# ScalarE instead of GpSimd writes the high parts of the product weights in an encoder layer's recurrence

## The chip, the core and the metric

The kernel is one program on one core of a Trainium2 chip. A core has TensorE (PE, with its weight loads shown as PEld), VectorE (DVE), ScalarE (ACT), GpSimd (POOL) and SyncE (SP), which here only starts transfers. The metric is the time of one execution on the device in microseconds, the median of several runs.

## What is computed

One layer, depth 1, batch 1, 1024 positions, 1024 channels, all float32. A single projection of x feeds a windowed attention, a recurrent branch and two merge gates:

```python
proj = einsum('bsd,de->bse', x, w_in) + b_in
q, k, v, g_attn, x_rnn, g_rnn, m_attn, m_rnn = split(proj)
attn = _window_attention(rope(q), rope(k), v, sink) * silu(g_attn)
xc = _centred_depthwise_conv(x_rnn, conv_w, conv_b)
rnn = _bidirectional_rglru(xc, ...) * silu(g_rnn)
merged = sigmoid(m_attn) * (attn @ w_branch_attn) + sigmoid(m_rnn) * (rnn @ w_branch_rnn)
x = layernorm(ALPHA * x + merged @ w_out + b_out)
```

The recurrence, for ten blocks of 128 channels and two directions:

```python
r = sigmoid(xb @ wa + ba); i = sigmoid(xb @ wx + bx)
log_a = -8 * r * softplus(-lam)
a = exp(log_a); u = sqrt(-expm1(2 * log_a)) * (i * x)
h = a * h + u      # forward over the positions, and backward; both are summed
```

## The kernel before

**Products in three parts.** Every matrix is split into a high part (the value as TensorE's fp32r type holds it) and a low part (the value less its high part). A product is high by high, high by low and low by high: three matmuls of 128 x 128 by 128 x 512. Weights arrive by DMA in `raw` or `raw_half`, one instruction makes `w_hi` and a second, a subtraction on POOL, makes `w_lo`.

**Stages.** Opening projection and attention run first, then (from about 430 us) the recurrence's first two blocks in plain form, then, from 461 us to 820 us, the stage that the change touches, and at the end the branch products, the output projection and the LayerNorm.

**The stage of the change.** Two units of 128 output columns are computed together as a "twin". By sums of the moving matrix that were made earlier, and sums of the weights, a twin takes seven half products instead of eight (Strassen's scheme with Winograd's sums). There are 16 twins (`TWINS`), so 112 half products, numbered n = 7q + i: twin q, product i from 0 to 6. One product is 12 matmuls (`product`, L1067 to L1082). Twins whose units are merge gates (`MERGES`) alternate with those that project x and the gate of a coming block.

The loop is over the blocks b = 2 to 9. In block b PE runs (L1143 to L1154): `gates(b, 0)`, product 0 of the block's twin q, `gates(b, 1)`, products 1 to 6 of q, then products 0 to 6 of the merge twin m. The two gate steps are 12 matmuls each, so a block has 16 such slots. Block 2 runs four products of q ahead of `gates(b, 1)`. Block 9 has no twin q, only m. Below, "q6" is product 6 of a block's twin q, "m0" product 0 of its merge twin, and so on.

**Weights of a product.** There are six landing places for raw halves (`half_slot`) and four for split weights (`w_slot`). A high part may be written once product n-3 has begun (`product_begun`, L1436 for ACT and L760 for POOL). The tuple `BY_ACT` says which of the 112 high parts ACT makes (`high_weights`, L1432, an ACTIVATE copy, counted in `act_hi_done`); all others are made by POOL in `split_half` (L763). POOL makes every low part (`low_weights`, L750), in the order of n. PE waits for it at L1070. SP loads the next raw half into a place when its low part is done (L606).

Before the change `BY_ACT` names products 2 to 9, and products 4, 5 and 6 of each merge twin but the last.

**What ACT does beside.** ACT's instructions for a block are written out by hand in a fixed order (L1546 to L1616): `early_copy(q, number)` takes partial products out of PSUM, number 3 after product 6; `sigmoids(b, 0)` and `(b, 1)` evacuate the gates; `decay_tanh`, `decay_exp`, `decay_square` and `roots` build the recurrence's coefficients; `conv_begin` and `conv_high` serve the next block's convolution; `merge_gate` applies the sigmoid of a merge gate and stores it by DMA; `sigmoid_of` makes the sigmoid for the gate of the branch. ACT changes its function table three times a block (ACT_TABLE_LOAD).

**What DVE does.** Also in fixed order (L1987 to L2026): `twin_sum` puts parts of a twin together (it waits for `early_done`), `gated_input`, `conv_tap`, `one_less_decay`, `scan_input`, `silu_of` (it waits for `sigmoid_of`), `scans` (two TENSOR_TENSOR_SCAN), `gated_sum`, which ends a block (`rnn_done`), and ACT's `sigmoids(b + 1, 0)` waits for that.

Both orders are coupled: ACT waits for DVE at `merge_gate`, `conv_begin` and `sigmoids`; DVE waits for ACT at `silu_of`, `one_less_decay`, `scan_input` and `twin_sum`.

Of the kernel before, what the change touches and what calls it, by code (L numbers as in the profile page):

```python
# [109 lines left out]
PLAIN = 1  # L110
TWINS = []
# [5 lines left out]
MERGES = tuple(q for q, twin in enumerate(TWINS) if twin[0][0] == "merge")  # L117
# [4 lines left out]
FIRST_PRESUM = 4  # L122


BY_ACT = (2, 3, 4, 5, 6, 7, 8, 9) + tuple(7 * q + i for q in MERGES[:-1] for i in (4, 5, 6))
ORDER = ((0, 0), None, (0, 1), None, (1, 1), None, None)
SUM_AT = {1: 0, 3: 1, 5: 3, 6: 2}

# [52 lines left out]
def encoder_layer(nc, x_t, x_rows, stream, small, tables, sink, b_out, ln_gain, ln_bias, out):  # L181
# [4 lines left out]
    with ctx:  # L186
# [521 lines left out]
        def _(pool):  # L708
# [43 lines left out]
            def split_half(n):  # L752

                pool.wait_ge(half_landed[n % N_SLOTS], 16 * (n // N_SLOTS + 1))
                if n in BY_ACT:
                    pool.wait_ge(act_hi_done, BY_ACT.index(n) + 1)
                    low_weights(n, half_slot(n % N_SLOTS))
# [462 lines left out]
        def _(act):  # L1220
# [130 lines left out]
            def conv_high(b):  # L1351
                act.wait_ge(convolved, b + 2)
                copy(conv_hi[:, :], conv[:, :]).then_inc(conv_hi_done, 1)
# [25 lines left out]
            def decay_tanh(b):  # L1379

                for d in range(2):
                    act.wait_ge(gate_freed[d], b * 2 + 3)
                    nc.scalar.activation(root[d][:, :], decay[d][:, :], ACT.Tanh,
                                         scale=rate[:, ds(b + d * RNN_BLOCKS, 1)]).then_inc(act_tanh, 1)

            def decay_exp(b, d):

                act.wait_ge(act_tanh, b * 2 + d + 1)
                nc.scalar.activation(decay[d][:, :], decay[d][:, :], ACT.Exp,
                                     scale=nrate[:, ds(b + d * RNN_BLOCKS, 1)]).then_inc(act_decay, 1)  # L1390

            def decay_square(b, d):

                act.wait_ge(act_decay, b * 2 + d + 1)
                if d == 1:
                    act.wait_ge(one_less, b * 2 + 1)
                elif b:
                    act.wait_ge(state_stored, 16 * b)
                nc.scalar.activation(square[:, :], decay[d][:, :], ACT.Square).then_inc(squared, 1)  # L1399
# [22 lines left out]
            def early_copy(q, number):  # L1422

                i, bank, at = ((0, 0, 0), (1, 2, 1), (3, 0, 2), (6, 0, 0))[number]
                act.wait_ge(product_done, 7 * q + i + 1)
                if number == 3:
                    act.wait_ge(twin_done, 4 * q + 1)
                elif q:
                    act.wait_ge(twin_done, 4 * (q - 1) + (4, 3, 2)[number])
                copy(early[:, at, :], twin_banks(q)[bank]).then_inc(early_done, 1)  # L1430

            def high_weights(q, i):  # L1432

                n = 7 * q + i
                act.wait_ge(half_landed[n % N_SLOTS], 16 * (n // N_SLOTS + 1))
                act.wait_ge(product_begun, max(1, n - 2))  # L1436
                copy(w_slot(n)[0], half_slot(n % N_SLOTS)).then_inc(act_hi_done, 1)

            def merge_gate(q, number):

                d, at = MERGES.index(q), number % 2
                gate_no, half = ((0, 0), (0, 1), (1, 1), (1, 0))[number]
                act.wait_ge(twin_done, 4 * q + number + 1)
                nc.scalar.activation(stage_out[:, at, :], stage_out[:, at, :], ACT.Sigmoid).then_inc(merge_gated, 1)
                act.wait_ge(merge_gated, 4 * d + number + 1)
                col = d * SEQ + half * HALF
                act.dma_start(merges[gate_no, :, col:col + HALF], stage_out[:, at, :])\
                    .then_inc(merge_stored[at], 16)
# [97 lines left out]
            for b in range(PLAIN + 1, RNN_BLOCKS):  # L1546
                last_one = b == RNN_BLOCKS - 1
                q, m = twin_of(b), merge_of(b)
                merge_before = merge_of(b - 1)
                if merge_before is not None:  # L1550
                    early_copy(merge_before, 3)
                if b == PLAIN + 1:
                    early_copy(q, 0)
                act.wait_ge(rnn_done, b)
                sigmoids(b, 0)
                if b == PLAIN + 1:
                    store_state(PLAIN)
                    early_copy(q, 1)
                    early_copy(q, 2)
                if merge_before is not None:  # L1560
                    merge_gate(merge_before, 2)
                    merge_gate(merge_before, 3)
                if q is not None and b > PLAIN + 1:
                    early_copy(q, 0)
                if last_one:
                    early_copy(m, 0)
                if not last_one:
                    conv_begin(b + 1, None)
                sigmoids(b, 1)
                if q is not None and b > PLAIN + 1:  # L1570
                    early_copy(q, 1)
                if last_one:
                    early_copy(m, 1)
                decay_tanh(b)
                decay_exp(b, 0)
                if not last_one:
                    decay_square(b, 0)
                decay_exp(b, 1)
                if b > PLAIN + 1:
                    early_copy(m if last_one else q, 2)  # L1580
                if last_one:
                    h_high(0)
                    h_high(1)
                    decay_square(b, 0)
                    merge_gate(m, 0)
                else:
                    conv_high(b + 1)
                decay_square(b, 1)
                if q is not None:
                    early_copy(q, 3)  # L1590
                if last_one:
                    merge_gate(m, 1)
                    early_copy(m, 3)
                    h_high(2)
                    h_high(3)
                roots(b)
                if last_one:
                    merge_gate(m, 2)
                    merge_gate(m, 3)
                    sigmoid_of(b)  # L1600
                    h_high(4)
                    h_high(5)
                    store_state(b)
                    for t in range(6, RNN_BLOCKS):
                        h_high(t)
                    break
                early_copy(m, 0)
                high_weights(m, 4)
                sigmoid_of(b)
                early_copy(m, 1)  # L1610
                high_weights(m, 5)
                high_weights(m, 6)
                early_copy(m, 2)
                merge_gate(m, 0)
                store_state(b)
                merge_gate(m, 1)  # L1616
# [609 lines left out]
```

## Time and profile before

| | |
|---|---|
| median of 3 runs | 1028.35 us (1027.28 to 1028.55) |
| the profiled execution | 1026.91 us, of which the span of its instructions 1025.1 us |
| busy: PE, PEld | 1005.0 us (98%), 831.5 us (81%) |
| busy: DVE, ACT, POOL | 687.3 us (67%), 476.4 us (46%), 650.5 us (63%) |
| granted TensorE clock, mean | 0.999 |
| HBM traffic | 112.55 MB read, 47.19 MB written |
| from 480.75 to 820.31 us | gate steps and products of blocks 2 to 9 |

The trace gives, for each engine, when an instruction ran and what its wait was for. Matmuls overlap: one of 128 x 512 shows 0.39 us, while the next starts 0.227 us after it. A busy PE in the table is therefore not a measure of its speed; the distance of starts is. In the busy shares of the whole span the stages are mixed: POOL is busy for three to six tenths of most slices of the attention, and for nearly all of the stage of the change.

### The profile page before, as it was taken

What the parts mean: (1) busy time and instruction counts of PE and PEld (TensorE: products, weight loads), DVE (VectorE), ACT (ScalarE), POOL (GpSimd) and SP (SyncE); (2) the same over time, 40 slices, a digit from 0 to 9 for tenths busy, and PEclk for the clock granted to TensorE, in tenths of its full rate; (3) what the DMA queues carried; (4) which work ended last, traced back from release to release, by engine and by line L of the source; (5) the groups of instructions that cost most, each with busy time, mean ns of one, the idle gap of its engine ahead of it and who ended that gap; (6) DMA issues with size and microseconds to landing.
All of it is one profiled execution on the core that took longest, in us unless ns stands there. A gap on an engine that the chain in (4) does not pass through costs nothing. (4 is left out here: it accounts for less than half of the span.)

```text
span 1025.1 us, 13044 instructions
## 1 busy us (share of the span) xinstructions
PE 1005.0 (98%) x4617; PEld 831.5 (81%) x4617; DVE 687.3 (67%) x776; ACT 476.4 (46%) x700; POOL 650.5 (63%) x399
## 2 busy tenths in 40 slices
PE   8999999999999999999999999999999999999997
PEld 6888888888888888888777788787887878888885
DVE  4946665603556653739788776978878588839756
ACT  4054455211554464775748566574855751102021
POOL 5654535545644534447999999999999733485223
PEclk9999999999999999999999999999999999999999
DMA  8264333575433431455352434435243788937012
GB/s 329 95 246 168 130 103 124 206 249 173 144 121 113 143 125 54 180 188 171 96 159 69 153 107 139 120 117 164 84 144 85 237 304 325 333 104 294 1 49 116
DMA packets 69605, 160.45 MB, mean 157 GB/s; under 512 B 7344, under 2 KB 7728, under 8 KB 69424
## 3 DMA queue, kind: packets, MB, share of 16 engines
q1 hardware_dynamic: 60624, 137.13, 40.6%
q10 hardware_dynamic: 8928, 22.64, 5.7%
q8 instruction: 31, 0.51, 0.2%
q14 instruction: 22, 0.18, 0.1%
HBM read 112.55 MB, written 47.19 MB: 156 GB/s over the span
## 5 line engine op out<-in xcount | busy, mean ns | idle before, releaser
L715 POOL TENSOR_SCALAR w_hi<-raw 128x1024 fp32r<-128x1024 f32 (+1 forms) x42 | 51.9, 1236 | 206.6 <-PE proj L870 146.7
L870 PE MATMUL proj<-xt_hi,w_hi 128*128 128x512 f32 x412 | 167.1, 406 | 1.4 <-DVE stage_out L1643 0.9
L872 PE MATMUL proj<-xt_hi,w_lo 128*128 128x512 f32 x412 | 161.5, 392 | 0.0
L871 PE MATMUL proj<-xt_lo,w_hi 128*128 128x512 f32 x412 | 161.3, 392 | 0.0
L750 POOL TENSOR_TENSOR w_lo<-raw,w_hi 128x512 fp32r<-128x512 f32 x76 | 148.2, 1955 | 8.9 <-ACT w_hi L1232 4.3
L718 POOL TENSOR_TENSOR w_lo<-raw,w_hi 128x1024 fp32r<-128x1024 f32 (+1 forms) x42 | 111.8, 2661 | 3.5
L1074 PE MATMUL proj<-xt_hi,w_hi 128*128 128x512 f32 x256 | 100.5, 393 | 3.0 <-POOL w_lo L750 2.8
L1080 PE MATMUL proj<-xt_hi,w_lo 128*128 128x512 f32 x256 | 99.8, 390 | 0.0
L1078 PE MATMUL proj<-xt_lo,w_hi 128*128 128x512 f32 x256 | 99.7, 389 | 0.0
L872 PEld LDWEIGHTS proj<-xt_hi,w_lo 128*128 128x128 f32 x412 | 77.3, 188 | 17.1
L870 PEld LDWEIGHTS proj<-xt_hi,w_hi 128*128 128x128 f32 x412 | 77.6, 188 | 14.1 <-DVE stage_out L1643 1.3
L871 PEld LDWEIGHTS proj<-xt_lo,w_hi 128*128 128x128 f32 x412 | 77.6, 188 | 11.6
L1278 ACT ACTIVATE probs<-masked,neg_max 128x385 f32<-128x385 f32 (+1 forms) x64 | 38.0, 593 | 93.6 <-DVE neg_max L1722 85.9
L1074 PE MATMUL proj<-t_hi,w_hi 128*128 128x512 f32 x192 | 75.3, 392 | 1.8 <-POOL w_lo L750 1.7
L1080 PE MATMUL proj<-t_hi,w_lo 128*128 128x512 f32 x192 | 74.8, 390 | 0.0
L1078 PE MATMUL proj<-t_lo,w_hi 128*128 128x512 f32 x192 | 74.7, 389 | 0.0
L750 POOL TENSOR_TENSOR w_lo<-raw_half,w_hi 128x512 fp32r<-128x512 f32 x36 | 67.7, 1883 | 4.3 <-ACT w_hi L1232 1.9
L763 POOL TENSOR_SCALAR w_hi<-raw 128x512 fp32r<-128x512 f32 x55 | 63.8, 1159 | 9.2 <-PE proj L870 7.3
L1879 DVE TENSOR_TENSOR_SCAN state<-decay,state 128x1024 f32<-128x1024 f32 x20 | 61.9, 3135 | 0.0
L1074 PEld LDWEIGHTS proj<-xt_hi,w_hi 128*128 128x128 f32 x256 | 48.0, 188 | 17.0 <-issue 7.1
L1643 DVE SCALAR_TENSOR_TENSOR root<-square,root 128x1024 f32<-128x1024 f32 x20 | 36.7, 1833 | 33.0 <-ACT square L1399 33.0
L1643 DVE SCALAR_TENSOR_TENSOR conv<-padded,par,conv 128x1024 f32<-128x1024 f32 x30 | 49.6, 1655 | 13.5 <-ACT conv L1347 12.9
(200 smaller groups left out, 2527.9 us busy)
## 6 DMA issues: line engine op xcount, KB each, us to landing
raw<-stream SPq DMA_DIRECT2D x48, 512.0 KB, 4.6
presum_a<-stream SPq DMA_DIRECT2D x48, 256.0 KB, 3.0
sums<-presum_a SPq DMA_DIRECT2D x48, 256.0 KB, 2.0
raw<-sums SPq DMA_DIRECT2D x44, 256.0 KB, 2.6
raw<-stream SPq DMA_DIRECT2D x34, 256.0 KB, 2.7
spill<-part ACTq DMA_DIRECT2D x16, 512.0 KB, 3.4
merges<-stage_out ACTq DMA_DIRECT2D x32, 256.0 KB, 2.6
raw_half<-stream SPq DMA_DIRECT2D x24, 256.0 KB, 2.7
```

The source lines that it names most:

```text
L715: nc.gpsimd.tensor_scalar(hi, raw[:, raw_slot, cols], 1.0, 0.0, ALU.mult, ALU.add)\
L718: nc.gpsimd.tensor_tensor(lo, raw[:, raw_slot, cols], hi.bitcast(f32), ALU.subtract)\
L750: nc.gpsimd.tensor_tensor(lo, src, hi.bitcast(f32), ALU.subtract).then_inc(product_split, 1)
L763: nc.gpsimd.tensor_scalar(w_slot(n)[0], half_slot(n % N_SLOTS), 1.0, 0.0, ALU.mult, ALU.add)\
L870: begun = nc.tensor.matmul(bank, wh, mov_hi, start=first, stop=False)
L871: nc.tensor.matmul(bank, wh, mov_lo, start=False, stop=False)
L872: return begun, nc.tensor.matmul(bank, wl, mov_hi, start=False, stop=last)
L1074: first = nc.tensor.matmul(bank, wh[:, c], moving[0][:, k, :], start=opens and k == 0, stop=False, skip_group_check=True)
L1078: nc.tensor.matmul(bank, wh[:, c], moving[1][:, k, :], start=False, stop=False, skip_group_check=True)
L1080: last = nc.tensor.matmul(bank, wl[:, c], moving[0][:, k, :], start=False, stop=k == KT // 2 - 1, skip_group_check=True)
L1643: return nc.vector.scalar_tensor_tensor(dst, a, scalar, b, op0, op1)
L1879: last = nc.vector.tensor_tensor_scan(state[d][:, ::turn], decay[d][:, ::turn], state[d][:, ::turn], 0.0, ALU.mult, ALU.add)
```

## The change

`BY_ACT` becomes the range 2 to 106, so ACT makes 105 high parts where it made 29. The 76 new ones are written into ACT's order at fixed places. POOL keeps seven high parts (products 0 and 1, and 2 to 6 of the last twin), all low parts and both parts of the gate weights.

```diff
--- before.py
+++ after.py
@@ -122,7 +122,7 @@
 FIRST_PRESUM = 4
 
 
-BY_ACT = (2, 3, 4, 5, 6, 7, 8, 9) + tuple(7 * q + i for q in MERGES[:-1] for i in (4, 5, 6))
+BY_ACT = tuple(range(2, 7 * (len(TWINS) - 1) + 2))
 ORDER = ((0, 0), None, (0, 1), None, (1, 1), None, None)
 SUM_AT = {1: 0, 3: 1, 5: 3, 6: 2}
 
@@ -1551,16 +1551,23 @@
                     early_copy(merge_before, 3)
                 if b == PLAIN + 1:
                     early_copy(q, 0)
+                    high_weights(q, 3)
                 act.wait_ge(rnn_done, b)
                 sigmoids(b, 0)
                 if b == PLAIN + 1:
                     store_state(PLAIN)
                     early_copy(q, 1)
+                    high_weights(q, 4)
+                    high_weights(q, 5)
                     early_copy(q, 2)
+                    high_weights(q, 6)
+                elif not last_one:
+                    high_weights(q, 2)
                 if merge_before is not None:
                     merge_gate(merge_before, 2)
                     merge_gate(merge_before, 3)
                 if q is not None and b > PLAIN + 1:
+                    high_weights(q, 3)
                     early_copy(q, 0)
                 if last_one:
                     early_copy(m, 0)
@@ -1569,9 +1576,12 @@
                 sigmoids(b, 1)
                 if q is not None and b > PLAIN + 1:
                     early_copy(q, 1)
+                    high_weights(q, 4)
                 if last_one:
                     early_copy(m, 1)
                 decay_tanh(b)
+                if q is not None and b > PLAIN + 1:
+                    high_weights(q, 5)
                 decay_exp(b, 0)
                 if not last_one:
                     decay_square(b, 0)
@@ -1584,10 +1594,15 @@
                     decay_square(b, 0)
                     merge_gate(m, 0)
                 else:
+                    if b > PLAIN + 1:
+                        high_weights(q, 6)
                     conv_high(b + 1)
+                    high_weights(m, 0)
                 decay_square(b, 1)
                 if q is not None:
+                    high_weights(m, 1)
                     early_copy(q, 3)
+                    high_weights(m, 2)
                 if last_one:
                     merge_gate(m, 1)
                     early_copy(m, 3)
@@ -1604,6 +1619,7 @@
                     for t in range(6, RNN_BLOCKS):
                         h_high(t)
                     break
+                high_weights(m, 3)
                 early_copy(m, 0)
                 high_weights(m, 4)
                 sigmoid_of(b)
@@ -1611,6 +1627,8 @@
                 high_weights(m, 5)
                 high_weights(m, 6)
                 early_copy(m, 2)
+                high_weights(m + 1, 0)
+                high_weights(m + 1, 1)
                 merge_gate(m, 0)
                 store_state(b)
                 merge_gate(m, 1)
```

What this does to the instruction orders is shown at three places. The first is ACT in a middle block (block 4), from `early_copy(q, 1)` to the second `decay_square`, which lies in time around products q2 to q6. Before:

```order
L1232 ACTIVATE early<-proj 128x512
L1383 ACTIVATE root<-decay,rate 128x1024 x2
L1389 ACT_TABLE_LOAD
L1389 ACTIVATE decay<-decay,nrate 128x1024
L1399 ACTIVATE square<-decay 128x1024
L1389 ACTIVATE decay<-decay,nrate 128x1024
L1232 ACTIVATE early<-proj 128x512
L1232 ACTIVATE conv_hi<-conv 128x1024
L1399 ACTIVATE square<-decay 128x1024
```

and now:

```order
L1232 ACTIVATE early<-proj 128x512
L1232 ACTIVATE w_hi<-raw 128x512
L1383 ACTIVATE root<-decay,rate 128x1024 x2
L1232 ACTIVATE w_hi<-raw_half 128x512
L1389 ACT_TABLE_LOAD
L1389 ACTIVATE decay<-decay,nrate 128x1024
L1399 ACTIVATE square<-decay 128x1024
L1389 ACTIVATE decay<-decay,nrate 128x1024
L1232 ACTIVATE early<-proj 128x512
L1232 ACTIVATE w_hi<-raw_half 128x512
L1232 ACTIVATE conv_hi<-conv 128x1024
L1232 ACTIVATE w_hi<-raw 128x512
```

Three copies `w_hi` have come in: for q4 ahead of the tanh, q5 behind it, and q6 behind `early_copy(q, 2)`; a fourth, for m0, follows `conv_high`. The one for m1 follows the last row shown.

The second place is ACT in the same block from `early_copy(q, 3)`, the first row, to `sigmoid_of`, the last. Before:

```order
L1232 ACTIVATE early<-proj 128x512
L1405 ACT_TABLE_LOAD
L1405 ACTIVATE root<-root 128x1024 x2
L1232 ACTIVATE early<-proj 128x512
L1232 ACTIVATE w_hi<-raw_half 128x512
L1463 ACT_TABLE_LOAD
L1463 ACTIVATE stage_out<-silu_g 128x1024
```

and now:

```order
L1232 ACTIVATE early<-proj 128x512
L1232 ACTIVATE w_hi<-raw 128x512
L1405 ACT_TABLE_LOAD
L1405 ACTIVATE root<-root 128x1024 x2
L1232 ACTIVATE w_hi<-raw 128x512
L1232 ACTIVATE early<-proj 128x512
L1232 ACTIVATE w_hi<-raw_half 128x512
L1463 ACT_TABLE_LOAD
L1463 ACTIVATE stage_out<-silu_g 128x1024
```

The copies for m2 and m3 are new; the one for m4 was there. Further on, outside these rows, the copies for q0 and q1 of the next block stand ahead of `merge_gate(m, 0)`, that for q2 behind `sigmoids(b, 0)`, and that for q3 behind the two merge gates.

The third place is POOL, where the weights of block 2's products are split. Before:

```order
L763 TENSOR_SCALAR w_hi<-raw_half 128x512
L750 TENSOR_TENSOR w_lo<-raw_half,w_hi 128x512
L763 TENSOR_SCALAR w_hi<-raw_half 128x512
L750 TENSOR_TENSOR w_lo<-raw_half,w_hi 128x512
L763 TENSOR_SCALAR w_hi<-raw 128x512
L750 TENSOR_TENSOR w_lo<-raw,w_hi 128x512
L763 TENSOR_SCALAR w_hi<-raw 128x512
L750 TENSOR_TENSOR w_lo<-raw,w_hi 128x512
L784 TENSOR_SCALAR gates_hi<-raw_half 128x512
L787 TENSOR_TENSOR gates_lo<-raw_half,gates_hi 128x512
```

and now:

```order
L750 TENSOR_TENSOR w_lo<-raw_half,w_hi 128x512 x2
L750 TENSOR_TENSOR w_lo<-raw,w_hi 128x512 x2
L784 TENSOR_SCALAR gates_hi<-raw_half 128x512
L787 TENSOR_TENSOR gates_lo<-raw_half,gates_hi 128x512
```

Each TENSOR_SCALAR that wrote `w_hi` is gone; the subtractions stand one behind another, and the two instructions on the gate weights stay where they were between products. SP's, DVE's and PE's orders are as before.

## Rows read from the trace of the kernel before

**Rows 1.** The page: busy time of each engine.

```profile
PE 1005.0 (98%) x4617; PEld 831.5 (81%) x4617; DVE 687.3 (67%) x776; ACT 476.4 (46%) x700; POOL 650.5 (63%) x399
```

**Rows 2.** The waits of PE: line, who was waited for, total us, times, longest.

```profile
PE proj L1074 <- POOL w_lo L750: 4.5, 11, 1.0
...
PE aux L870 <- ACT state L1375: 1.0, 1, 1.0
```

**Rows 3.** Busy time of each engine in two stretches (microseconds, instructions), PE clock, DMA.

```profile
596.52:640.04 43.52, 43.52 (x194) 36.04 (x192) 35.51 (x23) 26.44 (x32) 41.05 (x27) 1.00 0.41 125
729.35:773.45 44.10, 43.87 (x193) 35.81 (x192) 35.37 (x23) 27.79 (x34) 42.60 (x28) 1.00 0.42 126
```

**Rows 4.** The largest group of high parts on POOL, 480 to 821 us, as in part 5 of the page.

```profile
L763 POOL TENSOR_SCALAR w_hi<-raw 128x512 fp32r<-128x512 f32 x53 | 62.5, 1180 | 2.0 <-PE proj L1074 2.0
```

**Rows 5.** Timeline of PE: start, duration, line, operation, tiles, count, idle time before.

```profile
480.75 0.39 PE L870 MATMUL aux<-conv_hi,gates_hi 128*128 128x512 f32 x1
...
549.97 0.39 PE L1074 MATMUL proj<-xt_hi,w_hi 128*128 128x512 f32 x1
...
748.85 0.47 PE L1074 MATMUL proj<-xt_hi,w_hi 128*128 128x512 f32 x1 [0.23 <-POOL w_lo L750]
...
773.45 0.39 PE L1074 MATMUL proj<-xt_hi,w_hi 128*128 128x512 f32 x1
...
820.31 0.39 PE L870 MATMUL aux<-xt_hi,w_hi 128*128 128x512 f32 x1
```

**Rows 6.** Timeline of ACT, one stretch of blocks 5 and 6, then of blocks 7 and 8.

```profile
642.96 0.60 ACT L1232 ACTIVATE early<-proj 128x512 f32<-128x512 f32 x1 [1.54 <-PE proj L1080]
...
683.25 1.05 ACT L1232 ACTIVATE conv_hi<-conv 128x1024 fp32r<-128x1024 f32 x1
...
732.26 0.60 ACT L1232 ACTIVATE early<-proj 128x512 f32<-128x512 f32 x1 [2.75 <-PE proj L1080]
...
752.04 0.63 ACT L1444 ACTIVATE stage_out<-stage_out 128x512 f32<-128x512 f32 x1 [3.11 <-DVE stage_out L1643]
...
760.86 1.25 ACT L1347 ACTIVATE conv<-padded,par 128x1024 f32<-128x1024 f32 x1 [1.96 <-DVE state L1640]
...
771.65 1.05 ACT L1232 ACTIVATE conv_hi<-conv 128x1024 fp32r<-128x1024 f32 x1
```

**Rows 7.** Timeline of DVE, the same stretch of blocks 7 and 8.

```profile
739.59 1.48 DVE L1640 TENSOR_TENSOR silu_g<-silu_g,stage_out 128x1024 f32<-128x1024 f32 x1 [0.75 <-ACT stage_out L1463]
741.00 3.38 DVE L1879 TENSOR_TENSOR_SCAN state<-decay,state 128x1024 f32<-128x1024 f32 x1
...
748.18 1.61 DVE L1640 TENSOR_TENSOR state<-state 128x1024 f32<-128x1024 f32 x1
```

**Rows 8.** Timeline of ACT: one copy of a high part, and two in a row.

```profile
468.39 0.61 ACT L1232 ACTIVATE w_hi<-raw_half 128x512 fp32r<-128x512 f32 x1
...
517.48 1.14 ACT L1232 ACTIVATE w_hi<-raw 128x512 fp32r<-128x512 f32 x2
```

**Rows 9.** Timeline of POOL: low parts behind an ACT copy, beside scans, and alone.

```profile
469.15 1.90 POOL L750 TENSOR_TENSOR w_lo<-raw_half,w_hi 128x512 fp32r<-128x512 f32 x1 [1.66 <-ACT w_hi L1232]
...
745.43 3.28 POOL L750 TENSOR_TENSOR w_lo<-raw,w_hi 128x512 fp32r<-128x512 f32 x1
748.68 1.59 POOL L763 TENSOR_SCALAR w_hi<-raw 128x512 fp32r<-128x512 f32 x1
...
753.17 1.29 POOL L750 TENSOR_TENSOR w_lo<-raw,w_hi 128x512 fp32r<-128x512 f32 x1
```

**Rows 10.** Timeline of ACT, block 2 into block 3.

```profile
513.62 0.60 ACT L1232 ACTIVATE early<-proj 128x512 f32<-128x512 f32 x1 [0.78 <-DVE silu_g L1643]
...
549.57 1.04 ACT L1232 ACTIVATE conv_hi<-conv 128x1024 fp32r<-128x1024 f32 x1
```

**Rows 11.** Timeline of DVE: an addition in block 2, scans after the last block.

```profile
526.22 2.31 DVE L1640 TENSOR_TENSOR state<-state 128x1024 f32<-128x1024 f32 x1
...
839.79 2.28 DVE L1879 TENSOR_TENSOR_SCAN state<-decay,state 128x1024 f32<-128x1024 f32 x1
```

## The prediction

> **What bounds the kernel now.** I read the page first, for the engines' shares. PE is busy for 1005.0 of the span's 1025.1 us [rows 1], so nothing that only relieves another engine can bring more than PE's idle time. The waits of PE come next: it waited 4.5 us in total on POOL's low parts, in 11 waits, and 1.0 us once on ACT's evacuation of the gates [rows 2]. Then two stretches, each from the start of product q6 of one block to that of the next [rows 3]. The first has no wait of PE: 43.52 us for 16 slots (14 products, two gate steps), which is 2.72 us a slot. The second takes 44.10 us. In it POOL is busy for 42.60 us and ACT for only 27.79. It looks as if POOL were full and ACT had 16 us to spare.
>
> A share says nothing about when. So I followed ACT through one block on its timeline [rows 6] and DVE on its own [rows 7]. After product q6 ACT takes `early_copy(q, 3)` (732.26, it had waited for PE), the roots, a copy and `sigmoid_of`. DVE waits for that 0.75 us, then runs `silu_of`, two scans, the sum of the states and its product with the gate (from 739.59, the sum at 748.18). ACT waits for DVE (752.04), evacuates the gates, and waits for DVE again before `conv_begin` (760.86). Then come sigmoid, tanh, exp and square without a gap, until `early_copy(q, 2)` and `conv_high` at 771.65. That is a chain of 39.39 us from 732.26 which neither PE nor POOL shortens. Two blocks earlier the same stretch is 683.25 - 642.96 = 40.29 us [rows 6]. I take the mean, 39.84. Each block's chain starts when its q6 is done and ends near the next q6. ACT's idle time in the block is waiting inside this chain, or behind its end.
>
> **What the change takes away.** 76 high parts leave POOL. The largest group of them shows a mean of 1180 ns [rows 4], so the 11 of a middle block free about 13 of POOL's 42.6 us. POOL's lateness at m6 (748.85 starts late, [rows 5]) goes. All slots from 480.75 to 820.31 [rows 5] are 121, at 2.72 us they would be 329.1, and they take 339.6. Of the 10.4 us between, about 1.1 belong to the wait on ACT [rows 2]. So at most 9.3 us can be won.
>
> **What it adds.** ACT gains 76 copies. One shows 0.61 us, two in a row 1.14, so one more in a busy run costs 1.14 - 0.62 = 0.52 us [rows 8]. Of the 11 in a block, those for q0, q1 and q3 fall into ACT's waits for DVE, and q2 stands where a DVE wait before `conv_begin` follows (1.96 us, [rows 6]): I cost them at nothing. If DVE were quicker there, q2 and q3 would cost 0.5 each. The copies for m0 and m1 stand behind q6's, where ACT then waits for PE to finish q6 (2.75 us before 732.26): also nothing, as long as PE is behind. Copies for m2, m3, q4 and q5 stand in the chain itself with no wait between, 4 x 0.52 = 2.08 us. And the copy for q6 stands at its end.
>
> **The place that decides** is that last one. Before, POOL made q6's high part whenever its landing place allowed, independent of ACT's chain. Now the copy for q6 is queued on ACT behind tanh, a table load, exp, square, exp and `early_copy(q, 2)`. From the start of `early_copy(q, 3)` in the previous block:
> - the chain of blocks 7 and 8, the shorter of the two in [rows 6]: 39.39, plus the four copies 2.08, plus the copy itself 0.62;
> - ACT to POOL: 468.39 + 0.61 = 469.00, POOL starts 469.15, so 0.15 [rows 8, 9];
> - the low part, 1.29 alone [rows 9]. DVE at this moment has just ended `one_less_decay` and waits for `conv_high`, hence the undisturbed value;
> - POOL to PE: 745.43 + 3.28 = 748.71, PE starts 748.85, so 0.14 [rows 9, 5].
>
> That is 43.67 us. But PE wants q6 at 773.45 - 732.26 = 41.19 [rows 5, 6]. It comes 2.5 us late even in the shorter chain, with nothing behind it that could catch up: the next chain starts when q6 is done. The new period is this sum with the mean chain 39.84 in it, 44.12, plus 2.91 from the start of q6 to the next `early_copy(q, 3)` (729.35 to 732.26, [rows 3, 6]): **47.0 us a block**.
>
> **The sum.**
> 1. Block 2 into 3. ACT is behind there by itself. m0 to m3 come into a run without waits, 2.08 us, of which a wait of 0.78 before 513.62 [rows 10] takes some back: +1.30. With q4 and q5 (1.04) the copy for q6 starts at 549.57 + 2.34 = 551.91 [rows 10], and PE at 551.91 + 0.62 + 0.15 + 1.29 + 0.14 = 554.1, not 549.97 [rows 5]: +4.1. PE will show one long wait at m0 of block 2 too, up to 5 us, since m0's copy now follows `conv_high`. It lies beside the same chain and isn't added.
> 2. Blocks 3 to 8, five periods: 5 x 47.0 = 235.2, before 773.45 - 549.97 = 223.5 [rows 5]: +11.7.
> 3. After q6 of block 8: the late start at m6 is gone, -0.4 (its share of the 0.58 by which the stretches of [rows 3] differ). Block 9 has no copy of this kind; 0.
>
> Together +15.4. Against the profiled execution (1026.91 us) it gives 1042.3. The median is 1.4 above that execution, so 1043.8 there.
>
> **Bounds.** The low part beside DVE shows up to 3.28 [rows 9]; some 0.85 more in each of six blocks is +5. Below: DVE's scans show 3.38 beside POOL and 2.28 without it [rows 7, 11]. If less POOL work freed both scans of a block, the chain would be 2.2 shorter and the period 44.8: -11 against the sum, leaving +4. I take neither, because in the new order the low parts of m5, m6 and the next q0 still stand against the scans (their copies end just before).
>
> A rule bears on that. An addition on DVE shows 1.61 where POOL had a high part beside it (748.18 and 748.68), and 2.31 in another block where a low part ran [rows 7, 9, 11]. By the Trainium skill ("SBUF — State Buffer", section "SBUF: two separate sides") the port pair that DVE and GpSimd share is an exclusive lock, held for the whole instruction. So what DVE loses is the length of the one instruction ahead of it, and a row of low parts costs it more than low and high in turn. By that rule the sum and the product behind the scans lose time, and the total would be near 1050. By the idea that contention follows POOL's busy share it would be near 1033.
>
> **The rivals.**
> - **Low parts in a row hold DVE up.** For: POOL's backlog at the scans now has low parts only. Two operations a block (the sum, L1885, and the product behind it, L1892) at 2.31 instead of 1.61 are 1.4, some of it absorbed at `conv_begin`: 0.7 to 1.4 a block, six blocks, +4 to +8. 1048 to 1052.
> - **DVE gets free of POOL.** The row on scans without POOL speaks for it, the clustering of low parts against. The scans' loss gone, 2.2 us a block in five: 1043.8 - 11 = 1033, from 1030 to 1038.
> - **Faster: ACT's copies are in time.** If waits of ACT inside the chain absorb the four copies, and DVE shortens it by over a further microsecond, q6's weights are there before PE wants them, and only POOL's lateness disappears. It decides at 41.19 - 0.62 - 0.15 - 1.29 - 0.14 = 38.99 us from `early_copy(q, 3)` to the copy for q6, which is less than the chain now without any added copy (39.39). That speaks against it. If so, -9 us: 1019.
> - **It only trades one wait for another.** PE's new wait at q6 as long as the old ones on POOL: within 2 us of 1028. ACT would have to lose under 1 us a block; only the table loads' slack could give that, and there is none in [rows 6].
>
> **How the numbers follow.** Forecast (1039 to 1048) 0.60; low parts hold DVE up 0.14; DVE gets free 0.11; faster 0.09; a trade 0.06, of which 0.04 lie within 0.2%, about what a measurement here can tell from no change, and 0.02 above. The predicted time is the forecast's, 1043.8. From 1032 to 1052 the range takes in the forecast, the first rival and most of the second. Faster 0.09, same 0.04, slower 0.87.
>
> **What would show it.** In the waits of PE, w_lo L750 grows from 4.5 us to some 20, in few long waits: one at product q6 in each of blocks 3 to 8 of 2 to 4 us, one at m0 of block 2. At q6 POOL's low part was waiting for ACT's w_hi, so POOL is busy for under 30 us of a 47 us period, and ACT for some 34. The stretch from `early_copy(q, 3)` to the copy of q6 reads about 42 us. It would be wrong if PE ran from block to block in 43.5 us, if the long wait sat at another product, or if DVE's scans came down to 2.3 us.

## The result, and the profile after

| | before | after |
|---|---|---|
| median of 5 runs each | 1027.75 us (1025.99 to 1028.55) | 1043.76 us (1040.49 to 1044.92) |
| the profiled execution, its span | 1026.91, 1025.1 us | 1040.49, 1038.7 us |
| mean granted TensorE clock | 0.999 | 0.992 |

The ratio is 1.0146, with a 95% interval from 1.013 to 1.0161: slower by 16.0 us, by the medians, where 15.4 were forecast. The time is right; the sum behind it is right in part.

The page of the changed kernel: span, busy time of the engines (beside [rows 1]), and POOL's largest group of low parts, whose last two numbers are the idle time ahead of it and what ended most of that.

```profile
span 1038.7 us, 13120 instructions
...
PE 1009.5 (97%) x4617; PEld 837.5 (81%) x4617; DVE 676.6 (65%) x776; ACT 515.6 (50%) x776; POOL 554.4 (53%) x323
...
L750 POOL TENSOR_TENSOR w_lo<-raw,w_hi 128x512 fp32r<-128x512 f32 x76 | 145.2, 1920 | 78.8 <-ACT w_hi L1232 78.3
```

POOL is 96 us less busy and ACT 39 us more, as intended. It doesn't make the kernel faster: the largest group of low parts now stands behind 78.3 us of waiting for ACT's `w_hi`. The waits of PE, as in [rows 2]:

```profile
PE proj L1074 <- POOL w_lo L750: 15.0, 7, 4.2
...
PE proj L870 <- DVE stage_out L1661: 1.1, 1, 1.1
```

15.0 us against 4.5, and in 7 waits rather than 11. Six of them are at q6 of blocks 3 to 8, the seventh at m0 of block 2, where the prediction put them. Two of the six, in the timeline of PE:

```profile
553.15 0.47 PE L1074 MATMUL proj<-xt_hi,w_hi 128*128 128x512 f32 x1 [0.80 <-POOL w_lo L750]
...
785.71 0.47 PE L1074 MATMUL proj<-xt_hi,w_hi 128*128 128x512 f32 x1 [1.93 <-POOL w_lo L750]
```

Product q6 of block 3 starts at 553.15 and not at 549.97, that of block 8 at 785.71 and not at 773.45 [rows 5]. The stretches from q6 to q6 (of blocks 3, 6 and 7), with the columns of [rows 3]: length, busy time of PE, PEld, DVE, ACT and POOL, clock, DMA:

```profile
553.15:599.14 45.99, 43.93 (x193) 35.90 (x193) 34.56 (x24) 33.61 (x45) 30.35 (x16) 1.00 0.39 121
692.50:738.38 45.88, 43.88 (x192) 35.89 (x193) 34.19 (x24) 33.53 (x45) 30.05 (x16) 1.00 0.39 121
738.38:785.71 47.33, 45.40 (x193) 37.13 (x193) 33.77 (x24) 33.53 (x45) 29.35 (x16) 0.96 0.38 117
```

The periods of blocks 3 to 7 are 45.99, 45.80, 47.56, 45.88 and 47.33 us, where 47.0 was forecast for each. ACT is busy for 33.5 of them and POOL for about 30. The third stretch is 1.4 us longer, and the column that stands out in it is the granted clock, 0.96. At its beginning PE's matmuls run slowly. Shorter stretches show it: q6 of block 6, which is at full clock though PE had waited 2.05 us ahead of it too; the wait ahead of q6 of block 7; that q6 up to the start of `early_copy(q, 3)`; then q6 of block 8, and m0 of block 2 behind its wait of 4.22 us:

```profile
692.50:695.30 2.80, 2.80 (x12) 2.33 (x13) 2.80 (x2) 1.38 (x2) 2.75 (x2) 1.00 0.31 94
736.22:738.38 2.16, 0.16 (x1) 0.03 (x1) 1.33 (x2) 2.16 (x5) 1.27 (x1) 1.00 0.00 0
738.38:743.00 4.62, 4.62 (x13) 3.67 (x14) 3.16 (x2) 1.39 (x3) 4.25 (x2) 0.63 0.42 114
785.71:790.10 4.39, 4.39 (x12) 3.51 (x13) 3.16 (x2) 1.38 (x2) 4.24 (x2) 0.61 0.39 119
509.69:514.10 4.41, 4.41 (x12) 3.47 (x13) 4.41 (x4) 4.27 (x5) 3.78 (x2) 0.61 0.43 119
```

The product takes 2.80 us at clock 1.00, and about 4.4 of the 4.62 at 0.63; its first two matmuls start 0.50 us apart instead of 0.30, those behind them 0.43 instead of 0.23. Ahead of the slow one PE had been busy for 0.16 of 2.16 us. So a part of the loss isn't waiting but the lower of TensorE's two levels, 1.2 GHz instead of 2.4, for most of the 4.4 us after a wait. The prediction has no such term.

The chain itself, on ACT (the rows of [rows 6], one block):

```profile
743.00 0.60 ACT L1232 ACTIVATE early<-proj 128x512 f32<-128x512 f32 x1 [3.23 <-PE proj L1080]
...
764.25 0.63 ACT L1444 ACTIVATE stage_out<-stage_out 128x512 f32<-128x512 f32 x1 [3.79 <-DVE stage_out L1661]
...
771.71 1.24 ACT L1347 ACTIVATE conv<-padded,par 128x1024 f32<-128x1024 f32 x1
...
783.54 0.62 ACT L1232 ACTIVATE w_hi<-raw 128x512 fp32r<-128x512 f32 x1
```

on DVE (as in [rows 7]):

```profile
751.36 1.23 DVE L1658 TENSOR_TENSOR silu_g<-silu_g,stage_out 128x1024 f32<-128x1024 f32 x1 [2.41 <-ACT stage_out L1463]
752.50 3.41 DVE L1897 TENSOR_TENSOR_SCAN state<-decay,state 128x1024 f32<-128x1024 f32 x1
...
759.71 1.61 DVE L1658 TENSOR_TENSOR state<-state 128x1024 f32<-128x1024 f32 x1
761.36 2.20 DVE L1658 TENSOR_TENSOR square<-state,silu_g 128x1024 f32<-128x1024 f32 x1
...
767.51 0.75 DVE L1661 SCALAR_TENSOR_TENSOR stage_out<-proj,par,early 128x512 f32<-128x512 f32 x1 [0.73 <-PE proj L1080]
```

and on POOL, the low part of q6:

```profile
784.30 1.27 POOL L750 TENSOR_TENSOR w_lo<-raw,w_hi 128x512 fp32r<-128x512 f32 x1 [4.24 <-ACT w_hi L1232]
```

From `early_copy(q, 3)` at 743.00 to the copy for q6 at 783.54 it is 40.54 us. POOL had waited 4.24 us for that copy, and starts 0.14 behind it.

### The profile page after: what moved, and what is told of

Same layout as the page of the kernel before. It is cut to its first block, busy times and chain, and to the rows that moved or that the text cites. A ratio compares the mean times of both kernels' runs of the same rounds, so it can differ in the third digit from the quotient of the medians.

```text
span 1038.7 us, 13120 instructions
## 1 busy us (share of the span) xinstructions
PE 1009.5 (97%) x4617; PEld 837.5 (81%) x4617; DVE 676.6 (65%) x776; ACT 515.6 (50%) x776; POOL 554.4 (53%) x323
## 4 chain that ended last, share of the span: by engine, by line
PE 43%; ACT 4%; issue 2%; DVE 2%; POOL 1%; DMA 1%; DVEq 0%; ACTq 0%; POOLq 0%
PE proj L1074 7%; PE proj L1080 7%; PE proj L1078 7%; PE aux L870 3%; PE aux L872 3%; PE aux L871 3%; PE proj L870 2%; PE proj L872 2%; PE proj L871 2%; PE proj L1193 1%; PE aux L1191 1%; PE proj L1191 1%; PE aux L1193 1%; PE proj L1192 1%; PE aux L1192 1%
## 5 line engine op out<-in xcount | busy, mean ns | idle before, releaser
L750 POOL TENSOR_TENSOR w_lo<-raw,w_hi 128x512 fp32r<-128x512 f32 x76 | 145.2, 1920 | 78.8 <-ACT w_hi L1232 78.3
L870 PE MATMUL proj<-xt_hi,w_hi 128*128 128x512 f32 x412 | 167.4, 406 | 1.6 <-DVE stage_out L1661 1.1
L871 PE MATMUL proj<-xt_lo,w_hi 128*128 128x512 f32 x412 | 161.4, 392 | 0.0
L1074 PE MATMUL proj<-xt_hi,w_hi 128*128 128x512 f32 x256 | 103.2, 403 | 15.1 <-POOL w_lo L750 15.0
L1078 PE MATMUL proj<-xt_lo,w_hi 128*128 128x512 f32 x256 | 102.3, 399 | 0.0
L872 PEld LDWEIGHTS proj<-xt_hi,w_lo 128*128 128x128 f32 x412 | 77.4, 188 | 17.1
L750 POOL TENSOR_TENSOR w_lo<-raw_half,w_hi 128x512 fp32r<-128x512 f32 x36 | 65.8, 1831 | 46.0 <-ACT w_hi L1232 45.9
L870 PEld LDWEIGHTS proj<-xt_hi,w_hi 128*128 128x128 f32 x412 | 77.7, 188 | 14.8 <-DVE xt_lo L1658 1.7
L1661 DVE SCALAR_TENSOR_TENSOR conv<-padded,par,conv 128x1024 f32<-128x1024 f32 x30 | 54.5, 1816 | 14.4 <-ACT conv L1347 13.7
L1080 PEld LDWEIGHTS proj<-xt_hi,w_lo 128*128 128x128 f32 x256 | 49.7, 194 | 10.7
```

What stands on the lines that cost most here:

```text
L750: nc.gpsimd.tensor_tensor(lo, src, hi.bitcast(f32), ALU.subtract).then_inc(product_split, 1)
L870: begun = nc.tensor.matmul(bank, wh, mov_hi, start=first, stop=False)
L871: nc.tensor.matmul(bank, wh, mov_lo, start=False, stop=False)
L872: return begun, nc.tensor.matmul(bank, wl, mov_hi, start=False, stop=last)
L1074: first = nc.tensor.matmul(bank, wh[:, c], moving[0][:, k, :], start=opens and k == 0, stop=False, skip_group_check=True)
L1078: nc.tensor.matmul(bank, wh[:, c], moving[1][:, k, :], start=False, stop=False, skip_group_check=True)
```

## The experiments

**Theory.** The copies themselves cost little. What costs is that six of the 76, those for q6 of blocks 3 to 8, stand in ACT's queue at the end of the chain that is released by the previous q6. **Rivals:** ACT's greater load lengthens the chain wherever the copies stand; or low parts in a row hold DVE up.

### Six copies back to POOL

```diff
-BY_ACT = tuple(range(2, 7 * (len(TWINS) - 1) + 2))
+BY_ACT = tuple(n for n in range(2, 107) if n % 7 != 6 or n // 7 % 2 == 0 or n < 14)
             def high_weights(q, i):
...
+                if n not in BY_ACT:
+                    return
```

> The changed kernel with six of its 76 new copies given back to GpSimd: product q6's in blocks 3 to 8. My theory (the copy for q6 is queued at the end of ScalarE's chain, and that alone makes PE wait): the changed kernel's chain ends with early_copy(q, 2) at 40.6 us, before PE wants q6 at 41.2, so the long waits of PE at q6 and the slow matmuls behind them go. The wait at m0 of block 2 (4.4 us) stays. Time 1024 to 1029 us, 15 to 20 below the changed kernel. The rival (the loss is ScalarE's whole added load, 76 copies): six copies are a thirteenth of it, and the time falls by 1 to 2 us, to 1042.

Measured: 1028.95 us, 1.0009 of before (95% interval 0.9997 to 1.0021). The waits of PE:

```profile
PE proj L1074 <- POOL w_lo L750: 5.9, 6, 3.6
```

By the medians 14.8 of the 16.0 us hang on six copies of 76. The other 70 added copies remain, in the same ACT queue, and on balance cost at most some 2 us, by the interval. What is left of these waits lies at m0: 3.6 us in block 2, and 0.44 to 0.49 in blocks 4 to 8, since m0's copy stands behind `conv_high`. There is one more wait, of 1.54 us for POOL's gate weights at 483.02, that the trace of the kernel before doesn't have. This run is the strongest evidence for the place against the load.

### All copies on ACT, q6's one earlier

```diff
                     high_weights(q, 5)
+                    high_weights(q, 6)
                 decay_exp(b, 0)
...
-                    if b > PLAIN + 1:
-                        high_weights(q, 6)
                     conv_high(b + 1)
```

> All 76 copies stay on ScalarE; only q6's moves from behind early_copy(q, 2) to right behind q5's, ahead of the table load, the two exps and the square (blocks 3 to 8). My theory (position, not load): q6's weights are there about 5 us earlier; what then comes last for q6 is early_copy(q, 2), at 41.2 us from early_copy(q, 3), just when PE wants it. Waits at q6 under 0.5 us, time 1024 to 1030 us. The rival (load): nothing is lighter, 1042 to 1044 us.

Measured: 1031.26 us, 1.0026 (1.0015 to 1.0036), a little above what was expected. The waits of PE:

```profile
PE proj L1074 <- POOL w_lo L750: 6.8, 6, 4.7
PE proj L1074 <- ACT early L1232: 1.1, 3, 0.5
```

ACT does exactly what it does in the changed kernel, and 12.5 us are back: load is ruled out as the cause of these. What stays above before is in m0's waits (up to 4.7 us, in block 2), and a new one of up to 0.5 us: in blocks 4 to 6, q6 now has its weights and waits for `early_copy(q, 2)`, which the moved copy pushed back.

### Keeping PE busy during its wait

Ahead of its wait at q6, PE runs nine matmuls into a PSUM bank that is free at that time. Nobody reads them; the computation is otherwise whole.

```diff
                 if i == 6:
+                    if q % 2 and q > 1:
+                        b_now = (q + 3) // 2
+                        pe.wait_ge(gate_freed[0], 2 * b_now + 3)
+                        for _ in range(9):
+                            nc.tensor.matmul(aux[0][:, 0:HALF], w_slot(7 * q + 5)[0][:, 0:P], b22[0][:, 0, :],
+                                             start=True, stop=True)
```

> The changed kernel, with nine matmuls of 128 x 512 (about 2.0 us) of no use on PE ahead of its wait at q6 in blocks 3 to 8, into a PSUM bank that is free there. Theory of the clock (the granted clock of 0.61 to 0.67 in the 4 us behind three of these waits comes from PE's idling): with PE kept busy through the wait, q6's matmuls run at full clock in all six blocks, 1.4 to 1.7 us less in each block that was slow; 1036 to 1040 us, the granted clock above 0.995, and the runs closer together. The wait at m0 of block 2 may still be followed by a slow stretch. The rival (the slow matmuls have another cause, such as DMA or GpSimd beside them): 1042 to 1045 us and the same slow stretches.

Measured: 1040.39 us, 1.0112 (1.0093 to 1.0131), 0.4 us above the range. The stretches, with the columns of [rows 3], those of block 7's product q5 with the added matmuls, its q6, and q6 of block 8:

```profile
735.45:740.40 4.95, 4.92 (x23) 3.79 (x21) 2.59 (x3) 4.92 (x8) 1.30 (x1) 1.00 0.18 53
740.40:743.24 2.84, 2.84 (x13) 2.33 (x13) 2.84 (x2) 1.34 (x2) 2.83 (x2) 1.00 0.33 97
786.35:789.19 2.84, 2.84 (x13) 2.33 (x14) 2.84 (x2) 1.35 (x2) 2.82 (x2) 1.00 0.34 92
```

The added matmuls fill the wait, and q6 takes 2.84 us at clock 1.00 in all six blocks. But the condition also holds for the last twin, where there was no wait, and the nine cost 2.0 us there; and in block 3, where PE waits only 0.8 us, their 2.0 us were longer than the wait. So the gain stayed below what the slow stretches had cost. A second version puts no matmuls into the last twin, only four into block 3, and fills the long wait at m0 of block 2 too:

```diff
-                    if q % 2 and q > 1:
...
+                    if q % 2 and 1 < q < 14:
+                        fill(2 * ((q + 3) // 2) + 3, 7 * q + 5, b22, 4 if q == 3 else 9)
...
                 if i == 0:
+                    if q == 2:
+                        fill(7, 13, t3, 18)
```

> The changed kernel with idle time of PE filled more exactly than in e3: nine matmuls of no use ahead of q6 in blocks 4 to 8, four in block 3, none in block 9 (e3 had nine there, 2.0 us lost), and eighteen ahead of m0 in block 2. Theory of the clock: no slow stretch at all, granted clock 0.999, e3 less 2.0, less 1.0 in block 3, less 1.7 behind m0: 1035 to 1037 us. The rival (fills cost as much as they save): 1040 us as e3.

Measured: 1036.69 us, 1.0091 (1.0076 to 1.0107). Product q6 of blocks 7 and 8:

```profile
737.45:740.29 2.84, 2.84 (x12) 2.34 (x13) 2.84 (x2) 1.34 (x2) 2.82 (x2) 1.00 0.32 92
783.36:786.20 2.84, 2.84 (x13) 2.33 (x14) 2.84 (x2) 1.35 (x2) 2.82 (x2) 1.00 0.31 92
```

The periods are those of the changed kernel at full clock (q6 of block 3 starts at 553.22, that of block 8 at 783.36: 46.0 us each); PE spends the wait busily. So by the medians 1043.76 - 1036.69 = 7.1 us of the loss are the clock's, and 1036.69 - 1027.75 = 8.9 the wait's own. By the two ratios, 1.0146 and 1.0091, the clock's part is 5.7. The two profiled executions differ by 1040.49 - 1036.10 = 4.4 us, with three slow q6 in the first and none in the second. The slow stretch at m0 of block 2 is gone as well, and bought nothing: q6 of block 3 starts at 553.22 us here and at 553.15 there.

### The changed kernel a second time

> The changed kernel once more, for a second profile. Theory of the clock: which of the six waits at q6 are followed by a slow stretch differs from run to run; this profile has another number of them than three, and its time differs from 1040.5 us by about 1.7 us for each. The rival (the same three blocks each time): the same slow stretches at q6 of blocks 5, 7 and 8.

Measured: 1042.85 us, 1.0136 (1.012 to 1.0153). Its profiled execution took 1046.13 us, 5.6 more than the first. Product q6 in blocks 3 to 8:

```profile
554.62:557.45 2.83, 2.83 (x13) 2.33 (x13) 2.83 (x3) 1.36 (x2) 2.62 (x2) 1.00 0.49 120
600.47:604.89 4.42, 4.42 (x12) 3.47 (x13) 3.16 (x2) 1.39 (x2) 4.25 (x2) 0.61 0.42 119
648.12:652.52 4.40, 4.40 (x12) 3.50 (x13) 3.16 (x2) 1.38 (x2) 4.24 (x2) 0.61 0.41 119
695.96:700.36 4.40, 4.40 (x13) 3.50 (x13) 3.16 (x2) 1.38 (x2) 4.26 (x2) 0.61 0.42 119
743.37:747.79 4.42, 4.42 (x12) 3.48 (x13) 3.16 (x2) 1.39 (x2) 4.23 (x2) 0.61 0.38 119
790.85:795.18 4.33, 4.33 (x12) 3.38 (x13) 3.16 (x2) 1.37 (x2) 4.25 (x2) 0.62 0.41 121
```

In both profiles PE waits about 2 us ahead of q6 in blocks 4 to 8. All five of these q6 are slow here, in the first profile three (blocks 5, 7 and 8). With the clock at full, q6 takes 2.83 us, otherwise 4.33 to 4.42, so each costs 1.5 to 1.6, and two more of them account for 3.2 of the 5.6 us. A third lies outside the stage: in the first 20 us of the execution the granted clock is 0.91, in the first profile 1.00. Block 3, where PE waits 0.80 and 0.54 us, is at full clock in both. Why the same wait lowers the clock in one block and not in another stays open.

### Only what ACT has slack for

```diff
+BY_ACT = tuple(n for n in range(2, 107) if n < 14 or n > 104 or (n // 7 % 2 and n % 7 < 4)
+               or (n // 7 % 2 == 0 and n % 7 > 3))
```

(and the same guard as above). ACT keeps q0 to q3, m4 to m6 and all of block 2's q; POOL makes the rest.

> ScalarE makes only those high parts whose place in its order lies in one of its own waits: q0 to q3 and m4 to m6 in a block, and all of block 2's q. GpSimd makes q4 to q6 and m0 to m3 again (seven a block). My theory: the chain on ScalarE and DVE is as long as in the kernel before (39.4 to 40.3 us), so PE waits for neither, and GpSimd, with four high parts fewer a block, is no longer late at m6: periods of 43.5 to 43.8 us, 1018 to 1023 us. The rival (GpSimd's low parts, each held up by VectorE's operations, are late whatever it is relieved of): 1026 to 1028 us with waits at m6 as before.

Measured: 1036.52 us, 1.0078 (1.0057 to 1.0098): 13.5 us above the range, and above the rival's too. PE's waits, then POOL's timeline from block 7 into block 8:

```profile
PE proj L1075 <- POOL w_lo L751: 9.1, 23, 1.0
```

```profile
755.66 4.50 POOL L751 TENSOR_TENSOR w_lo<-raw,w_hi 128x512 fp32r<-128x512 f32 x2
764.06 1.30 POOL L751 TENSOR_TENSOR w_lo<-raw,w_hi 128x512 fp32r<-128x512 f32 x1 [3.90 <-ACT w_hi L1233]
767.22 1.53 POOL L751 TENSOR_TENSOR w_lo<-raw_half,w_hi 128x512 fp32r<-128x512 f32 x1 [1.85 <-ACT w_hi L1233]
```

PE has no long wait any more but 23 short ones, of up to 1.0 us, most at q4, m2 and m6. The rows suggest why. POOL works in order too. It stands idle for 3.90 and 1.85 us, because ACT's copies for q2 and q3 come late, and the low parts for these two come ahead of q4's high part in its order, though that is its own to make. In the changed kernel such idling is harmless, since POOL has 16 us to spare; here it has its high parts to do.

### The kernel before with six copies moved

```diff
+               + tuple(7 * q + 6 for q in range(3, 14, 2))))
...
+                    if b > PLAIN + 1:
+                        high_weights(q, 6)
                     conv_high(b + 1)
```

> The kernel before, with only the copy for q6 of blocks 3 to 8 moved to ScalarE, to the place it has in the changed kernel (behind early_copy(q, 2)); GpSimd makes all others as before. The sum of my prediction without the four copies in the chain: 39.84 + 0.62 + 0.15 + 1.29 + 0.14 + 2.91 = 44.95 us a block, where the kernel before takes 43.5 to 46.6: 1028 to 1031 us. The rival, which e4 suggests (GpSimd works in order, so a late copy makes it idle, and with high parts of its own behind it cannot catch up): m0 to m3 come late one after another, 1035 us or more.

Measured: 1036.48 us, 1.0088 (1.0072 to 1.0103), above the range. The waits of PE, then POOL's from 480 to 840 us:

```profile
PE proj L1075 <- POOL w_lo L751: 9.2, 19, 1.7
```

```profile
POOL w_lo L751 <- ACT w_hi L1233: 12.9, 5, 3.9
POOL w_lo L751 <- PE proj L1075: 8.2, 3, 2.7
```

The rival that the expectation names has come true. Six copies alone, 3.7 us of ACT's time, cost 8.7 us. PE waits 0.4 to 1.7 us at q6 of blocks 3, 5 and 7, and in the same blocks again at m3 to m5 (up to 1.0 us) and at m0 or m1: POOL has waited 3.1 to 3.9 us for ACT and then needs a high and a low part for each product. In blocks 4, 6 and 8 q6 isn't late; why every second block is spared stays open. The changed kernel's 70 further copies give POOL the room to catch up behind q6, and it has no such waits behind q6. It is slower still all the same: four of them a block stand in the chain, and it has slow stretches of the clock, which this one's stage doesn't.

### Better versions

The first experiment, with m0's copy ahead of `conv_high` too:

```diff
                 decay_tanh(b)
+                if b == PLAIN + 1:
+                    high_weights(m, 0)
...
+                    if b > PLAIN + 1:
+                        high_weights(m, 0)
                     conv_high(b + 1)
-                    high_weights(m, 0)
```

> e1 (q6's high parts of blocks 3 to 8 on GpSimd) with m0's copy moved forward on ScalarE: ahead of conv_high in blocks 3 to 8, right behind decay_tanh in block 2. In e1 PE still waited before m0: 3.7 us and a slow stretch of 1.7 behind it in block 2, 0.7 in four later blocks. My theory: these are again copies queued too far back, and go: 1018 to 1023 us, under the kernel before. The rival (m0 waits for something else, such as GpSimd's own order, or DVE's putting together): 1027 to 1029 us.

Measured: 1025.13 us, 0.9976 (0.9967 to 0.9985). The gain over before is 2.7 us, clear of zero by its interval and less than expected. PE's waits, and block 2's m0 and m1 on its timeline:

```profile
PE proj L1074 <- POOL w_lo L750: 3.6, 3, 3.2
```

```profile
507.30 0.47 PE L1074 MATMUL proj<-xt_hi,w_hi 128*128 128x512 f32 x1 [0.20 <-POOL w_lo L750]
...
513.45 0.47 PE L1074 MATMUL proj<-t_hi,w_hi 128*128 128x512 f32 x1 [3.17 <-POOL w_lo L750]
```

m0 comes in time, and 3.17 us of the wait have gone to m1. So m1's copy was moved as well:

```diff
                     high_weights(m, 0)
+                    high_weights(m, 1)
```

> b1 with the copy for m1 of block 2 moved forward as well, right behind that for m0 (behind decay_tanh). In b1 PE waited 3.4 us at m1 of block 2, since its copy stood behind the second decay_square. Position theory: that wait goes down to under 1 us and what follows in block 2 moves forward with it, 1021 to 1023 us. The rival (block 2's end is set by ScalarE's and VectorE's chain, which m1's wait only ran beside): 1024 to 1026 us, with the waits moved on to the gate steps or q6 of block 3.

Measured: 1025.10 us, 0.9965 (0.9952 to 0.9979). The waits of PE:

```profile
PE proj L1074 <- POOL w_lo L750: 2.9, 5, 1.6
```

0.7 us less waiting, and no gain that can be told: the medians are 1025.13 and 1025.10, and the two intervals overlap. The waits have gone on to m2 (0.67 us) and m3 (1.60) of block 2. The time is the rival's, the place of the waits neither's. That the chain on ACT and DVE sets the end of block 2 fits this, but with only 0.7 us taken away it isn't shown by it.

With all 76 on ACT, q6's copy early, and `early_copy(q, 2)` and m0's copy early too:

```diff
                     high_weights(q, 5)
+                    early_copy(q, 2)
                     high_weights(q, 6)
```

> e2 (all 76 copies on ScalarE, q6's right behind q5's) with early_copy(q, 2) moved forward too, between the copies for q5 and q6, and m0's copy forward as in b1. What e2 still lost was up to 0.7 us before q6 (early_copy) and before m0, and 4.9 and 2.5 us around m0 of block 2. My theory: all these go, and what is left is ScalarE's chain itself, now 3.1 us longer than before and closing on itself at 44 us a block: 1019 to 1025 us. The rival (with all copies ScalarE's total order is too long, and the waits only move on to early_copy(q, 3) or the gates): 1028 to 1031 us.

Measured: 1027.97 us, 1.0003 (0.9993 to 1.0013), 3 us above the range and at the rival's lower edge. The waits of PE:

```profile
PE proj L1074 <- POOL w_lo L750: 5.5, 8, 3.1
```

Each copy that is put ahead of the chain's work pushes the next one back: the waits are at m1 now, 0.3 to 0.4 us a block and 3.1 in block 2.

## Why the prediction was right, and where its sum wasn't

- **The place that decides: right.** Six of PE's seven waits are at q6, POOL's wait for ACT stands ahead of them (4.24 us at 784.30), and putting six copies back ends them.
- **Handovers: right.** 0.62 for the copy, 0.14 to POOL, 1.27 for the low part, 0.14 to PE (785.71 - 784.30 - 1.27).
- **Copies at nothing, 0.52 for those in the chain: right.** From `early_copy(q, 3)` to `silu_of` the block has 8.36 us (743.00 to 751.36) where it had 7.33 (732.26 to 739.59, [rows 6, 7]): 1.03 for m2 and m3. From `conv_begin` to the place of q6's copy it has 11.83 where it had 10.79 [rows 6]: 1.04 for q4 and q5.
- **"ACT's idle time is waiting inside this chain": the step that failed.** The prediction let the middle of the chain stand as it was. From the evacuation of the merge gate to `conv_begin` it was 8.82 us (752.04 to 760.86, with a wait of 1.96 in it, [rows 6]) and is 7.46 (764.25 to 771.71, with none), although q2 and q3 have come in. DVE was ready 1.36 us earlier. Before, it had waited there for the store of a merge gate:

```profile
756.43 0.75 DVE L1643 SCALAR_TENSOR_TENSOR stage_out<-proj,par,early 128x512 f32<-128x512 f32 x1 [1.42 <-DMA merges<-stage_out]
```

The store, issued behind the row at 752.04, landed after 3.6 us; the one behind the row at 764.25 landed after 2.5 us, and DVE then waited 0.73 us for PE instead (the row at 767.51). That is 1.13 of the 1.36 us (756.43 - 752.04 less 767.51 - 764.25), and 0.23 are two additions on DVE behind it, 3.44 us instead of 3.67. Why the store was quicker wasn't tried. Over blocks 3 to 8, DVE's waits for these stores fell from 7.6 to 2.0 us, and ACT's waits for DVE at `conv_begin` from 6.6 to 1.2. Between these two parts, from `silu_of` to the evacuation, the chain grew by 0.44 us (12.45 to 12.89), which the prediction had at nothing in its forecast. In all, 1.03 + 0.44 - 1.36 + 1.04 = 1.15: 39.39 us became 40.54, where the four copies alone would make 41.47, and 41.92 had been forecast from the mean chain. In the five periods this chain is 40.54 to 41.04 us. At full clock the period is about 45.9 us and not 47.0, so over five periods this term was some 5.6 us too large.
- **The clock: missing.** It gave nearly the same back: 7.1 us by the medians of the filled waits, 5.7 by the ratios. In the profiled execution three slow q6 are 1.6 us each.
- **The sum by its steps**, in the profiled execution. Block 2 into 3: +3.2 (forecast +4.1). Five periods: 785.71 - 553.15 = 232.6 against 223.5, +9.1 (forecast +11.7). After q6 of block 8: the stage ends at 833.65, which is 47.9 after, and 46.9 before: +1.1 (forecast -0.4), one slow q6 of 1.6 in it. Together +13.3. So it was luck that 15.4 came out near 16.0: two errors of opposite sign met.
- **The wait at m0 of block 2** is 4.2 us (up to 5 forecast) and lies beside the chain, as forecast: with its slow stretch filled away q6 of block 3 started no earlier (553.22 and 553.15 us).
- **Rival "DVE gets free": wrong.** The scan still takes 3.41 us.
- **Rival "low parts in a row": half right, and small.** The sum takes 1.61 us in every block. The product behind it (761.36) takes 2.20 us, in blocks 2 to 8 alike. In the kernel before one of the two took 2.2 to 2.3 in blocks 2 to 4, and neither in blocks 5 to 8 (1.61 and 1.52). So the rival's 1.4 us a block came out as 0.7, and in four blocks only. `silu_of` took some of it back, 1.23 instead of 1.48 us in this block, and the total did not go to 1050. The prediction's reading of the sum at 748.18 was off: POOL's low part ran until 748.71, and the high part (748.68) stood beside the sum's end and the product. The lock that the prediction cites from the Trainium skill ("SBUF — State Buffer", section "SBUF: two separate sides") agrees with these rows: the product takes 1.52 us where POOL had begun a high part of 1.59 us ahead of it, and 2.20 where it had begun a low part of 2.28 us (760.19). What it didn't settle is how many of the rows meet a low part.
- **"Faster"** failed as argued: the copy came 40.54 us behind `early_copy(q, 3)`, and 38.99 would have been needed.

## What to carry to other kernels

What an instruction costs in an in-order queue depends on the work that it stands behind and on who waits for it, more than on its length or the engine's busy share: here 70 moved copies cost nothing that could be told, and six cost 15 us. Ask too whose queue stands idle behind the late one, since taking part of a move back can leave an engine waiting that no longer has the time to. And where one idle gap is opened in the middle of PE's run, price its clock as well as its length.

## What the runs showed of the hardware

A wait of PE of about 2 us (1.93 to 2.06), with PE busy without a gap before it, was followed by a granted clock of 0.61 to 0.66 over about 4.4 us, which cost 1.5 to 1.6 us on top: three quarters of the wait. It happened at three of five such waits in one execution and at all five in another. With the 0.80 and 0.54 us of block 3 it did not. Longer waits were no surer sign: behind 4.2 us at m0 of block 2 it happened in both, and in two of the better versions, with a wait of 3.1 to 3.2 us at m1 of block 2, the clock was 1.00 behind it in the one (without q6's copies on ACT) and 0.62 in the other (all copies on ACT). With useless matmuls in the gap it did not occur at q6 at all (clock 0.995 to 0.999 over the execution, against 0.987 to 0.992).

The product behind the scans on DVE, 128x1024 with two inputs, took 2.20 us where GpSimd had begun a low part just ahead of it, and 1.52 us where it had begun a high part.
